# Two attentions of the second model: probabilities normalised ahead of the transposes, weighted with values stationary, output feature-major

## What is computed

```python
def ab_mixer(u, ...):
    ...
    ya = delta_mixer(qa, ka, va, za, ba, aa, conv_w, a_log, dt_bias, a_out_g)
    ...
    yb = window_mixer(qb, kb, vb, sink)          # 8 heads of 64, 2 key/value heads
    return jnp.concatenate([ya, yb.astype(ya.dtype)], axis=-1) @ w_out

def window_mixer(q, k, v, sink):
    ...
    p = jax.nn.softmax(jnp.concatenate([s_win, s_meta, s_sink], axis=-1), axis=-1)
    ...

def dense_mixer(q, k, v):                        # 8 heads of 128, 2 key/value heads
    ...
        s = jnp.einsum('bqkgd,bskd->bkgqs', qi, k).astype(jnp.float32)
        p = jax.nn.softmax(s, axis=-1).astype(v.dtype)
        return jnp.einsum('bkgqs,bskd->bqkgd', p, v)

def c_mixer(u, w_qkv, qg, kg, w_out, cos, sin):
    ...
    return dense_mixer(q, k, v) @ w_out
```

## Time and profile before

| | us |
|---|---|
| median of three runs | 2152.51 |
| the three runs | 2149.67, 2152.51, 2154.37 |
| span of the profiled execution | 2148.5 |
| window attention, first score to last output | 1190.6 to 1261.8 |
| dense attention, first score to last output | 1849.3 to 1893.3 |

### The profile page before, as it was taken

One profiled execution on the slowest core, in us unless ns is written; L12 is line 12 of the kernel. 1 busy time (PEld: TensorE's weight loads), 2 busy tenths in 40 slices (PEclk: granted clock), 3 DMA queues, 4 the chain that ended last, 5 costly groups with the idle time before them and its releaser, 6 DMA issues.

```text
span 2148.5 us, 22899 instructions
## 1 busy us (share of the span) xinstructions
PE 1800.0 (84%) x9259; PEld 1242.7 (58%) x9259; DVE 832.3 (39%) x1791; ACT 462.3 (22%) x813; POOL 0.4 (0%) x6
## 2 busy tenths in 40 slices
PE   7957999997885899998599875876799989687998
PEld 5644543443664444434274654874289984447998
DVE  6872110012215311100362455554355553515665
ACT  1131111110123011101111521210134330313443
POOL 0000000000000000000000000000000000000000
PEclk9967899998996799999789568887999998888999
DMA  8143389999132339999820000001425433101551
GB/s 279 45 171 111 117 310 395 391 395 343 39 117 99 104 124 388 395 395 392 309 83 0 1 1 0 1 1 53 182 88 187 156 131 143 40 0 40 187 205 59
DMA packets 153207, 348.01 MB, mean 162 GB/s; under 512 B 8096, under 2 KB 15136, under 8 KB 153136
## 3 DMA queue, kind: packets, MB, share of 16 engines
q1 hardware_dynamic: 145616, 338.28, 42.6%
q10 hardware_dynamic: 7520, 8.75, 1.3%
HBM read 345.97 MB, written 1.05 MB: 162 GB/s over the span
## 4 chain that ended last, share of the span: by engine, by line
PE 70%; DVE 11%; DMA 10%; ACT 3%; issue 3%; SPq 2%; DVEq 0%; ACTq 0%
PE ps L691 65%; DMA ring<-in_w_up 9%; DVE ring L1638 2%; SPq L602 2%; DVE arena L1638 2%; DVE h L1644 1%; DMA ring<-in_w_in 1%; PE ps L698 1%; PE ps L967 1%; ACT arena L1448 1%; PE ps L1010 1%; DVE small L1644 0%; ACT hT L1280 0%; DVE ring L1644 0%; ACT arena L1280 0%
## 5 line engine op out<-in xcount | busy, mean ns | idle before, releaser
L691 PE MATMUL ps<-ring,arena 128*64 128x512 f32 (+3 forms) x1656 | 377.4, 592 | 26.9 <-DMA ring<-in_w_up 23.4
L691 PE MATMUL ps<-ring,hT 128*128 128x512 f32 (+5 forms) x864 | 355.1, 572 | 9.4 <-DMA ring<-in_w_in 5.9
L691 PE MATMUL ps<-arena_r,ring_r 128*128 128x272 f32 (+1 forms) x1024 | 294.2, 287 | 0.0
L691 PEld LDWEIGHTS ps<-ring,arena 128*64 128x64 f32 (+1 forms) x1656 | 136.1, 144 | 252.9 <-issue 248.4
L691 PEld LDWEIGHTS ps<-ring,hT 128*128 128x128 f32 (+1 forms) x864 | 158.8, 186 | 198.6 <-issue 183.0
L1280 ACT ACTIVATE arena<-ps 128x256 f32<-128x256 f32 (+6 forms) x184 | 83.0, 478 | 622.0 <-PE ps L691 394.3
L691 PEld LDWEIGHTS ps<-arena_r,ring_r 128*128 128x128 f32 x1024 | 195.9, 191 | 0.0
L691 PE MATMUL ps<-arena_r,ff_hi_r 128*128 128x272 f32 (+1 forms) x992 | 186.2, 285 | 2.8 <-DVE arena L1638 2.8
L691 PE MATMUL ps<-arena_r,y_r 128*128 128x272 f32 (+1 forms) x544 | 152.5, 292 | 26.5 <-DVE ring_r L1638 23.4
L691 PE MATMUL ps<-ring 128*128 128x128 f32 (+2 forms) x848 | 133.8, 326 | 40.2 <-DVE ring L1638 30.3
L691 PE MATMUL ps<-arena 128*128 128x512 f32 (+9 forms) x464 | 131.5, 480 | 42.7 <-DVE small L1641 22.5
(11 more groups left out here) (264 smaller groups left out, 1716.4 us busy)
## 6 DMA issues: line engine op xcount, KB each, us to landing
ring<-in_w_down SPq DMA_DIRECT2D x32, 2048.0 KB, 14.5
ring<-in_w_gate SPq DMA_DIRECT2D x32, 2048.0 KB, 17.6
ring<-in_w_up SPq DMA_DIRECT2D x32, 2048.0 KB, 19.3
ring<-in_w_ff SPq DMA_DIRECT2D x32, 2048.0 KB, 8.0
ring<-in_w_in SPq DMA_DIRECT2D x8, 2048.0 KB, 19.5
ring<-in_w_in_ab SPq DMA_DIRECT2D x5, 2048.0 KB, 12.6
ring<-in_w_o SPq DMA_DIRECT2D x4, 2048.0 KB, 11.5
ring<-in_ple_gate SPq DMA_DIRECT2D x4, 2048.0 KB, 19.7
```

The source lines that it names most:

```text
L691: return pe.matmul(o, lhsT, rhs, start=a, stop=z)
```

## The change

The reciprocals are no longer applied to the output. VectorE multiplies the probabilities by them, head by head, ahead of the transposes (`shares`, four TENSOR_SCALARs of rows x 272), and signals `p_ready`, for which `turn` now waits in place of `s2_exp`. `weigh` swaps its operands: the values are the weights and the transposed probabilities move. In the dense attention one product per key block serves all four heads (512 columns); in the window attention two per block (256 columns each), for even and odd heads, whose 64 output features go to partitions 0 to 63 and 64 to 127. So bank 7 holds the output feature-major, and ScalarE copies it straight into `uT` (`outputs` on ScalarE, behind the pT copies of the next step). `project_out` loses its transposes; the twelve of `oacc` stay ahead of the first projection. `delta_inputs(i)` now stands behind shares(i). SyncE's first wait on `yT_mm` counts 3 in place of 5.

```diff
@@ -300,7 +300,6 @@
         vtok = view(1536, NT2 * A_W, pat="p (t h d) -> p t h d", t=NT2, h=A_H)
-        yb = tqb
         qp = y_t[:, 0:NT2 * B_QW].rearrange("p (t n) -> p t n", t=NT2)
@@ -487,6 +486,7 @@
         ATT_BASE = [0, len(ATT[0])]
+        P_BASE = [NT * DEPTH, NT * DEPTH + len(ATT[0])]
         base2 = [slot_count(n, DEPTH) for n in range(NSLOT)]
@@ -644,7 +644,7 @@
-                    sp.wait_ge(yT_mm, 5)
+                    sp.wait_ge(yT_mm, NT2)
                     ff_load(L, 0 + 1, 0, 1)
@@ -969,15 +969,8 @@
-            def project_out(n, srcs, tiles, full_of, slots):
-
-                for t in range(tiles):
-                    for c in range(KC):
-                        b, o = (2 * t + c // 4, (c % 4) * P) if t < NT else (4, c * N_META)
-                        ins = pe.transpose(ps[:, b, o:o + rows(t)], srcs(t, c), ident[0:rows(t), 0:rows(t)])
-                        if t == NT and c == KC - 1 or t < NT and c % 4 == 3:
-                            ins.then_inc(yT_mm, 1)
-                pe.wait_ge(yT_ev, n + 2 * NT + (tiles > NT))
+            def project_out(tiles, full_of, slots):
+
                 for half in range(2):
@@ -1004,7 +997,7 @@
                         pe.wait_ge(pT2_ev, base + i)
-                    pe.wait_ge(s2_exp, base + i + 1)
+                    pe.wait_ge(p_ready, P_BASE[which] + i + 1)
                     for b in range(NT2):
@@ -1017,9 +1010,13 @@
                         pe.wait_ge(o2_ev, base + i)
-                    for hd in range(GRP):
-                        for b in range(NT2):
-                            ins = mm(ps[0:r, 7, hd * kvw:(hd + 1) * kvw], pTs[i % 2][0:rows(b), b, hd, 0:r], v(b, g), b == 0, b == NT2 - 1)
+                    for b in range(NT2):
+                        if kvw == P:
+                            ins = mm(ps[:, 7, :], v(b, g), pTs[i % 2][0:rows(b), b, :, :], b == 0, b == NT2 - 1)
+                            continue
+                        for odd in range(2):
+                            o = ps[kvw * odd:kvw * odd + kvw, 7, 0:2 * r].rearrange("p (c s) -> p c s", c=2)
+                            ins = mm(o, v(b, g), pTs[i % 2][0:rows(b), b, odd::2, 0:r], b == 0, b == NT2 - 1)
                     ins.then_inc(o2_mm, 1)
@@ -1163,8 +1160,12 @@
             pe.wait_ge(mix2_ready, 1)
-            project_out(0, lambda t, c: oacc[0:rows(t), t, c * P:(c + 1) * P] if c < 4 else yb[0:rows(t), t, (c - 4) * P:(c - 3) * P],
-                        NT2, wo_full, (0, 1))
+            for t in range(NT2):
+                for c in range(A_H):
+                    ins = pe.transpose(ps[:, 2 * t, c * rows(t):(c + 1) * rows(t)], oacc[0:rows(t), t, c * P:(c + 1) * P], ident[0:rows(t), 0:rows(t)])
+                ins.then_inc(yT_mm, 1)
+            pe.wait_ge(yT_ev, NT2)
+            project_out(NT2, wo_full, (0, 1))
@@ -1264,7 +1265,7 @@
             pe.wait_ge(o2_ev, ATT_BASE[1] + len(ATT[1]))
-            project_out(5, lambda t, c: cq[:, t, c * P:(c + 1) * P], NT, [woc_full[4], woc_full[5]], (4, 5))
+            project_out(NT, [woc_full[4], woc_full[5]], (4, 5))
             feed_forward(1)
@@ -1448,17 +1449,6 @@
-            def to_yT(n, tiles):
-                for t in range(tiles):
-                    for half in range(2 if t < NT else 1):
-                        i = n + 2 * t + half
-                        act.wait_ge(yT_mm, i + 1)
-                        if t < NT:
-                            ins = copy(uT[:, 4 * half:4 * half + 4, cols(t)], ps[:, 2 * t + half, :].rearrange("p (c s) -> p c s", c=4))
-                        else:
-                            ins = copy(uT[:, :, cols(t)], ps[:, 4, 0:KC * N_META].rearrange("p (c s) -> p c s", c=KC))
-                        ins.then_inc(yT_ev, 1)
-
             def attend(which, probs, pTs, tile_rows, between=None):
@@ -1474,6 +1464,13 @@
+                def outputs(i):
+                    t, g = steps[i]
+                    n = GRP if which else GRP // 2
+                    c = n * g if which else A_H + n * g
+                    act.wait_ge(o2_mm, base + i + 1)
+                    copy(uT[:, c:c + n, cols(t)], ps[:, 7, 0:n * tile_rows(t)].rearrange("p (c s) -> p c s", c=n)).then_inc(o2_ev, 1)
+
                 exps(0)
@@ -1485,6 +1482,9 @@
                         between(i)
+                    if i > 0:
+                        outputs(i - 1)
+                outputs(len(steps) - 1)
@@ -1567,7 +1567,9 @@
                 copy(vnew[d], heads(ps[:, 4 + d, :])).then_inc(vn_ev, 1)
-            to_yT(0, NT2)
+            for t in range(NT2):
+                act.wait_ge(yT_mm, t + 1)
+                copy(uT[:, 0:A_H, cols(t)], ps[:, 2 * t, 0:A_H * rows(t)].rearrange("p (c s) -> p c s", c=A_H)).then_inc(yT_ev, 1)
@@ -1622,7 +1624,6 @@
             attend(1, c_prob, c_pT, rows)
-            to_yT(5, NT)
             feed_forward(1)
@@ -2017,7 +2018,7 @@
-            def attend(which, probs, dst, kvw, tile_rows, between=None):
+            def attend(which, probs, tile_rows, between=None):
                 steps, base = ATT[which], ATT_BASE[which]
@@ -2049,25 +2050,18 @@
                     link(dve.reciprocal(rs2[0:r, c], sm2[0:r, c]))
-
-                def outputs(i):
-                    t, g = steps[i]
-                    r, c = tile_rows(t), slice(4 * i, 4 * i + 4)
-                    dve.wait_ge(o2_mm, base + i + 1)
-                    o = dst[0:r, t, 4 * g * kvw:4 * (g + 1) * kvw].rearrange("p (h d) -> p h d", h=GRP)
-                    tt(o, ps[0:r, 7, 0:4 * kvw].rearrange("p (h d) -> p h d", h=GRP),
-                       rs2[0:r, c].unsqueeze(2).to_broadcast([r, GRP, kvw]), ALU.mult).then_inc(o2_ev, 1)
+                    for hd in range(GRP):
+                        n = 4 * i + hd
+                        ins = ts(probs[i % 2][0:r, hd, :], probs[i % 2][0:r, hd, :], rs2[0:r, n:n + 1], None, ALU.mult)
+                    ins.then_inc(p_ready, 1)
                     if between:
...
                 masked(0)
-                for i in range(len(steps) + 1):
+                for i in range(len(steps)):
                     if i + 1 < len(steps):
                         masked(i + 1)
-                    if i < len(steps):
-                        shares(i)
-                    if i > 0:
-                        outputs(i - 1)
+                    shares(i)
@@ -2156,7 +2150,7 @@
-            attend(0, w_prob, yb, B_HD, rows, delta_inputs)
+            attend(0, w_prob, rows, delta_inputs)
@@ -2345,7 +2339,7 @@
             dve.tensor_copy(tA[:, 0:1], rstd2[:, 0:1]).then_inc(qn_ready, 1)
-            attend(1, c_prob, cq, C_HD, rows)
+            attend(1, c_prob, rows)
             add_tiles(NT, lambda half, t: dve.wait_ge(wo_mm, 6 + 2 * half + t + 1), lambda half, t: 3 * half + t)
```

## The result

| | runs | median us | range us | against the kernel before, same chip |
|---|---|---|---|---|
| before, first session | 16 | 2152.49 | 2146.26 to 2154.82 | |
| changed | 16 | 2158.78 | 2155.04 to 2165.03 | ratio 1.0033 [1.0023, 1.0043] |
| changed, once more | 12 | 2154.74 | 2150.92 to 2164.29 | ratio 1.0012 [0.9992, 1.0033] |

The change costs 0.33% in the first session, which is more than the 0.2% that a measurement tells from no change, and 0.12% in the second, which is less. The two intervals overlap between 1.0023 and 1.0033. 2158.8 us lies inside the stated range of 2148.5 to 2164 and 3.5 us above the number forecast; the first session's verdict, slower, is the one that had 0.36, not the one that had 0.52, and the second session's is no change.

A forecast was written before the change was run, and what follows sets the result against it. TensorE, busy 84% of the span, was taken to bound the kernel, with nothing else running beside the two attentions. Terms 3.0 - 1.2 + 2.1 - 1.1 = +2.8 gave 2155.3 us, no change that can be told; range 2148.5 to 2164.

The forecast's parts named there:

- Part 2: Both attentions: VectorE's shares, 1.6 and 1.4 us, now precede the transposes; turn(i) follows mask(i+1), one ring without overlap.
- Part 1: Weigh in both attentions: fewer products; window 1.33 us high clock, 2.65 low, against 6.5; dense 2.65 high, 5.3 low.
- C: Slower rival, window attention: weigh's two column halves do not overlap in short bursts, +10.6 on top, 2166 us; chance 0.06.
- The window attention's +3.0: End of mask(1) to first transpose behind the window attention, 57.7 us before: +3.0 with every turn low, two scores high.
- Its projection's -1.2: Projection after the window attention: -2.3 us from twelve fewer transposes, 1.1 given back through a longer low-clock stretch.
- The dense attention's +2.1: End of mask(1) to first projection matmul in the dense attention: 36.8 us before, 38.9 with mixed clock.
- all low: The dense attention's sum with everything at the low clock: 50.4 us, +13.6.
- The dense projection's -1.1: Dense projection's low-clock start: the high clock would save 2.15 us; half counted, as dense weighs now precede it.
- A: Slower rival: both attentions' rings stay mostly at the low clock; full price +19, taken +9, 2161.5 us; chance 0.24.
- D: Faster rival: high clock holds from each weigh into the projection; -14 at most, half-way -5, 2147.5 us; chance 0.12.
- B: Slower rival: transposes do not raise the clock, in both attentions; +13.5 us, 2166; chance 0.06.

The follow-up runs named there:

- window only: The kernel before with the change in the window attention and its projection only: 2155.50 us, ratio 1.0024 to the kernel before.
- multiplied twice: The changed kernel with four more multiplications per step, by 1.0, behind the four by the shares: 2165.49 us, ratio 1.0054 to the kernel before.
- dense only: The kernel before with the change in the dense attention and its transposes only: 2151.93 us, ratio 1.0007 to the kernel before.
- the fifth experiment: The changed kernel with shares(i), then the delta work, both ahead of the next step's mask: 2139.05 us, ratio 0.9940 to the kernel before.
- the first variant: The changed kernel with shares(i) ahead of the next step's mask and the delta work behind that mask: 2131.24 us, ratio 0.9907 to the kernel before.

## Where the prediction was right, and where it failed

- **The mechanism stands.** Part 2 said that turn(i) would come behind mask(i+1) and that the step would become one ring without overlap. The chain of waits shows just that, the pauses are 5.0 to 5.5 and 4.2 to 4.3 us (4 to 5 forecast), all large turns in the window attention and three of four in the dense one are at the low clock, and doubling the multiplications lengthened eight pauses by 0.5 to 1.0 us each and the time by 9 to 11 us. The mask of step 2 started 6.9 us behind the end of mask(1), not 8.2: score(2) ran high, and the delta work, which the prediction called covered, ended just after it and was the last thing that this mask waited for, by some 0.4 us.
- **Part 1 stands.** The weigh of the window attention took 1.66 to 3.02 us (1.33 or 2.65 forecast), so the two column halves run side by side and C, which asked for about 5 us, is out. Both prices were 0.3 too low; with 32 moving columns it took 1.00 (1.2 taken). Six dense instructions took 2.93 at the high clock, 0.3 above the price taken. The multiplications took 1.18 for four (1.2 taken).
- **The window attention's +3.0** measured +1.4 as a difference of two means whose members lie 3 to 5 us apart. Nothing here tells +3.0 and +1.4 apart.
- **Its projection's -1.2** measured -2.2 from the transposes and +1.2 behind them, -1.0 in all: both halves of the term stand.
- **The dense attention's +2.1 was too low.** From the end of mask(1) to the first product of the projection both traces of the kernel before have 36.8 us, and the changed one 40.8 (1864.15 to 1904.96): +4.0. (The table has +3.1, since the second trace of the kernel before took 1.8 us more ahead of that point, its first score at the low clock.) The mix of clocks was nearly right: the two rounds took 10.3 and 13.3 us where 9.8 and 13.0 were forecast. The term that was sized worst is the tail, 17.2 for 16.1, and in it the price of six instructions of 512 columns: 2.93 and 3.01 us at the high clock, not 2.65, and 4.5 in the mixed one, not 4.0. In all, 40.8 for 38.9 is a sixth of the way to the "all low" sum, though by the price of the instructions more than by the clock.
- **The dense projection's -1.1** measured -2.2: the full price of the low stretch that it began with before, since the dense weighs now hand it the high clock (64 products in 27.73 us, above). The prediction took half.
- **A term was missing.** The delta rule's stretch, which the change does not touch, is +3.5 us of the +5.2 in the traces, the largest single term, and the prediction had it at nothing without saying so. In all thirteen traces its length goes with the moment at which the clock rose in it, and not with the form of the attention ahead of it. At its start the granted clock is 0.50 in each of them. Where it rose 4.1 to 4.2 us later, the stretch took 231.1 us (four traces: both of the changed kernel, window only, multiplied twice); where it rose 2.8 us later, 230.5 (dense only, whose window attention has the old form); where it rose 5.2 to 5.3 us later, 228.6 to 228.7 (the kernel before, and the fifth experiment); where it rose 5.5 to 6.0 us later, 226.2 to 226.6 (the six others, the second trace of the kernel before among them). The stretch's first work, 24 transposes, shows it: in the changed kernel it took 4.83 us, with the high clock in its last part (1262.77 above), and in the kernel before again, at the low clock throughout,

```profile
1260.11 5.35 PE L1079 MATMUL ps<-consts,arena 128*128 128x128 f32 x24 [0.60 <-DVE arena L1638]
```

By these readings the change acts on this stretch only by where it lets it begin against the changes of the clock. In the changed kernel that came out the same in both traces, in the four traces with the old form in three different ways. Why an earlier rise goes with a longer stretch is not shown.
- **The rivals.** A, the ring mostly low, had the sign that came out, at +9. The truth lies between the forecast and A: the window attention's granted clock was 0.66 and the dense one's 0.77, not below 0.6. The chances (0.52 for no change) stand about where two sessions leave the matter, 1.0033 and 1.0012. The lower end of the range, 2148.5, is 1 us above the 2147.5 that D's half-way price gives; the result does not touch it.
- **What was luck.** The four terms that the prediction had come to +1.3 us in the table (+1.4, -1.0, +3.1, -2.2), where it had +2.8. The rest of the +5.2 in the traces is the missing term and scatter. That the forecast lies within 4 us of the measured time was partly chance.
- **B, and the Trainium skill's rule.** In the changed kernel's first round TensorE stood idle for 5 us, did twelve transposes at a granted clock of 0.50 and nothing else, and ran the score behind them at 0.98 (windows above). In that trace three of the four large turns of the window attention had work at or near the high clock's price right behind them (a score in 2.2 us, weighs in 1.7), and one a weigh in 2.68. With the pauses filled, 24 transposes took 4.04 us, with the clock rising on the way, and the next 24 ran wholly at the high clock, 2.84. The Trainium skill, TensorE: Matmul & The Clock Gate, Part 4, says that transposes do not count as activity for the clock; these traces, like the one that the prediction read, disagree for these transposes in float32.
- **What the prediction did not ask.** It named the order that made the ring and took it as given. The order was worth more than any other term: the first variant has the changed kernel's instructions and is 23 to 27 us faster by the ratios, 20 below the kernel before.

## What to carry to other kernels

When an operation is moved from behind a product to ahead of it, look first at what is queued ahead of it on its own engine: here four multiplications, 1.2 us together in each step, cost in all 25 to 29 us behind the next step's mask and 1.5 ahead of it, which is nothing within the scatter. Other work for the same engine (the delta work) goes where that engine would wait anyway, beside the exponentials. And when a variant takes work off TensorE and the time stays, compare its pauses and what runs right behind them before calling the saving worthless.

## What the runs showed of the hardware

- A pause of 4.2 to 5.5 us was followed by twelve transposes at 1.2 GHz in all seven places where the changed kernel had one ahead of a large turn (2.8 us instead of 1.5). Filling five such pauses and one ahead of a small turn with useless transposes brought 10 us. But a long pause is not needed for the low clock: without the multiplications, the four large turns of the window attention took 2.82 us behind pauses of at most 1.6 us.
- Two traces of one program can differ by 3.3 us at one point and agree to 0.03 us at every later stage of the table: in the changed kernel the window attention took 68.8 and 72.1 us, and both ended at 1262.8. Against 1222.51 and 1224.10 above, the second trace has

```profile
1219.35 3.02 PE L691 MATMUL ps<-ring,arena 128*64 128x256 f32 x12
1222.31 3.99 PE L691 MATMUL ps<-ring 64*128 64x272 f32 x8
1231.36 2.79 PE L1003 MATMUL ps<-consts,ring 128*128 128x128 f32 x12 [5.07 <-DVE ring L1642]
```

It is 3.2 us ahead at the weigh and, with weigh and score at the low clock where the first trace had them at the high one, level with it (1231.27) at the next turn. A lead was lost to the clock: the length of a stage in one trace is a poor measure of its cost when the clock changes within it.
- Four TENSOR_SCALARs of 128x272 with a scalar per partition took 1.18 us, and with the constant 1.0 0.93 us.
